# The gated rows of a state-space scan: both tiles interleaved in a job of one step per chunk, with a scratch row for each tile

## What is computed

```python
y = y + d_skip[:, None] * xs
y = y.reshape(B, S, SSD_WIDTH) * silu(sz)                  # the gate
y_ssd = rms_norm(y.reshape(B, S, SSD_GROUPS, gsz), ssd_norm.reshape(SSD_GROUPS, gsz))
```

## Time and profile before

| | us |
|---|---|
| median of 3 runs (lowest to highest) | 3448.64 (3448.18 to 3449.01) |
| the profiled execution, device time | 3450.18 |
| its span in the trace | 3448.4 |
| PE busy / DVE busy / ACT busy | 3332.8 / 2236.4 / 1704.1 |
| mean granted PE clock | 0.984 |
| DMA moved, mean rate | 719.32 MB, 209 GB/s |

### The profile page before, as it was taken

One profiled execution on the slowest core, in us unless ns is written; L12 is line 12 of the kernel. 1 busy time (PEld: TensorE's weight loads), 2 busy tenths in 40 slices (PEclk: granted clock), 3 DMA queues, 4 the chain that ended last, 5 costly groups with the idle time before them and its releaser, 6 DMA issues.

```text
span 3448.4 us, 43913 instructions
## 1 busy us (share of the span) xinstructions
PE 3332.8 (97%) x18250; PEld 2894.4 (84%) x18250; DVE 2236.4 (65%) x2687; ACT 1704.1 (49%) x2098; POOL 46.8 (1%) x90
## 2 busy tenths in 40 slices
PE   5899999999999999999999999999999999999998
PEld 5779978888888887899788878888898899988887
DVE  5788777866667556776666576655567776544444
ACT  3355565554434344656646544344447775434343
POOL 0000000000000000000000000000000000000000
PEclk8799999999999999999999999999999999999999
DMA  9764456567777555444444467765555443455553
GB/s 367 274 228 170 167 226 245 218 228 259 263 277 295 208 183 183 175 168 160 172 182 159 176 239 270 265 250 192 189 184 191 182 165 135 166 216 194 194 187 142
DMA packets 102918, 719.32 MB, mean 209 GB/s; under 512 B 12176, under 2 KB 12256, under 8 KB 18752
## 3 DMA queue, kind: packets, MB, share of 16 engines
q1 hardware_dynamic: 93888, 675.38, 53.6%
q0 software_dynamic: 8256, 37.64, 3.1%
q10 hardware_dynamic: 576, 3.50, 0.3%
HBM read 710.08 MB, written 6.40 MB: 208 GB/s over the span
## 4 chain that ended last, share of the span: by engine, by line
PE 87%; DVE 7%; ACT 3%; issue 1%; DMA 1%; SPq 0%; DVEq 0%; ACTq 0%
PE G L1214 80%; DVE LL L1812 3%; DMA RAW<-w_ada_turned_packed_dram 1%; PE BD L1335 1%; PE BA L1362 1%; DVE S L2019 1%; PE BD L1397 1%; DVE RAW L1823 1%; ACT HH L1455 1%; PE BC L1348 1%; PE BE L1280 0%; PE BA L1416 0%; PE BC L1416 0%; PE BC L1380 0%; ACT WW L1734 0%
## 5 line engine op out<-in xcount | busy, mean ns | idle before, releaser
L1455 ACT ACTIVATE HH<-RAW 128x2048 fp32r<-128x2048 f32 x546 | 1044.8, 1914 | 1071.4 <-PE G L1214 1017.1
L1812 DVE TENSOR_TENSOR LL<-RAW,HH 128x2048 fp32r<-128x2048 f32 x546 | 1248.1, 2287 | 362.3 <-ACT HH L1455 361.9
L1214 PE MATMUL G<-HH,UH 128*128 128x512 f32 x2560 | 1021.1, 399 | 51.0 <-DVE LL L1812 46.7
L1214 PE MATMUL G<-HH,UL 128*128 128x512 f32 x2560 | 1003.2, 392 | 0.0
L1214 PE MATMUL G<-LL,UH 128*128 128x512 f32 x2560 | 1003.0, 392 | 0.0
L1214 PEld LDWEIGHTS G<-HH,UH 128*128 128x128 f32 x2560 | 484.7, 189 | 159.6 <-DVE LL L1812 56.2
L1214 PE MATMUL G<-UH,HH 128*128 128x256 f32 x2080 | 603.0, 290 | 10.2 <-DVE XS L2055 7.7
L1214 PE MATMUL G<-UH,LL 128*128 128x256 f32 x2080 | 589.3, 283 | 0.0
L1214 PE MATMUL G<-UL,HH 128*128 128x256 f32 x2080 | 589.1, 283 | 0.0
L1214 PEld LDWEIGHTS G<-LL,UH 128*128 128x128 f32 x2560 | 484.4, 189 | 103.3
L1214 PEld LDWEIGHTS G<-HH,UL 128*128 128x128 f32 x2560 | 485.2, 190 | 100.5 <-issue 2.9
(11 more groups left out here) (336 smaller groups left out, 2304.7 us busy)
## 6 DMA issues: line engine op xcount, KB each, us to landing
RAW<-in_w_in_packed_dram SPq DMA_DIRECT2D x402, 1024.0 KB, 4.8
RAW<-w_ada_turned_packed_dram SPq DMA_DIRECT2D x88, 1024.0 KB, 5.0
RAW<-in_w_out_packed_dram SPq DMA_DIRECT2D x48, 1024.0 KB, 4.8
RAW<-in_w_o_ssd_packed_dram SPq DMA_DIRECT2D x32, 1024.0 KB, 4.8
RAW<-in_w_o_fox_packed_dram SPq DMA_DIRECT2D x16, 1024.0 KB, 4.8
RAW<-in_w_o_dsa_packed_dram SPq DMA_DIRECT2D x16, 1024.0 KB, 5.7
RAW<-in_w_proj_a_packed_dram SPq DMA_DIRECT2D x16, 1024.0 KB, 4.8
RAW<-in_w_proj_b_packed_dram SPq DMA_DIRECT2D x16, 1024.0 KB, 4.7
```

The lines of the kernel that those rows point to most:

```text
L1214: mm = pe.matmul(to, lt, rh, start=first, stop=end, skip_group_check=True)
L1455: a.activation(HH[g % NH][:, :n], RAW[buf(ch["f"])][:, :n], ACT.Copy).then_inc(*hi_done.up(g))
L1812: v.tensor_tensor(LL[buf(f)][:, :n], RAW[buf(f)][:, :n], HH[g % NH][:, :n].bitcast(F32), ALU.subtract).then_inc(*lo_done.up(g))
```

## The change

The job `sz` still has five steps, none of them with MID. The two tiles go one behind the other: gate 0; gate 1 and norm 0; norm 1 and the transposes of 0; store 0 and the transposes of 1; store 1. After gate 1 the block's banks are declared free with sz_y of tile 1. Tile 1 gets its own scratch row XD in place of S1 and its own two columns of SM2, so that its gate waits for no event of the lane; its transposes wait until tile 0 has been stored, since both go through BE.

```diff
--- before.py
+++ after.py
@@ -407,15 +407,20 @@
     def sz(l, g):
         def steps(b):
             o.tok_block["sz", l, g] = b
-            for t in range(2):
-                put("sz_gate", l, g, t)
-                yield
-                put("sz_norm", l, g, t)
-                yield MID
-                put("sz_turn", l, g, t)
-                yield
-                put("sz_put", l, g, t)
-                ended("sz_done", l, g, t)
+            put("sz_gate", l, g, 0)
+            yield
+            put("sz_gate", l, g, 1)
+            o.blocks[b]["free_by"] = ("sz_y", l, g, 1)
+            put("sz_norm", l, g, 0)
+            yield
+            put("sz_norm", l, g, 1)
+            put("sz_turn", l, g, 0)
+            yield
+            put("sz_put", l, g, 0)
+            put("sz_turn", l, g, 1)
+            yield
+            put("sz_put", l, g, 1)
+            ended("sz_done", l, g, 1)
         return steps
 
     def gate(key):
@@ -874,6 +879,7 @@
     TURN = [(BA, BC), (BD, BE)]
     MT = [(BA, BC), (BD, BE), (BA, BC), (BD, BE)]
     SS = [S1, S2]
+    ZZ = [S1, XD]
     CV = [S1, S2]
     ROT = {"rot": (0, 16), "idx": (32, 8)}
     LW = [XD[:, :], XDD[:, :]]
@@ -1313,6 +1319,8 @@
 
         def sz_turn(l, g, t):
             pe.wait_ge(*sz_normed.at(l, g, t))
+            if t:
+                pe.wait_ge(*sz_done.at(l, g, 0))
             y = xsK[:, g, t, :]
             for j in range(4):
                 mm = pe.transpose(BE[:, j * P:(j + 1) * P], y[:, j * P:(j + 1) * P], ident)
@@ -1590,14 +1598,15 @@
         def sz_gate(l, g, t):
             b = o.tok_block["sz", l, g]
             a.wait_ge(*multiplied(b))
-            a.wait_ge(*evac_before("sz_gate", l, g, t))
-            a.activation(S1[:, :], GB[o.blocks[b]["set"]][t][:, :], ACT.Tanh, scale=0.5).then_inc(*sz_tanh.up(l, g, t))
+            if t == 0:
+                a.wait_ge(*evac_before("sz_gate", l, g, t))
+            a.activation(ZZ[t][:, :], GB[o.blocks[b]["set"]][t][:, :], ACT.Tanh, scale=0.5).then_inc(*sz_tanh.up(l, g, t))
 
         def sz_norm(l, g, t):
             a.wait_ge(*sz_y.at(l, g, t))
-            a.activation(S1[:, :], xsK[:, g, t, :], ACT.Square, accum_out=SM2[:, 0:1]).then_inc(*sz_sum.up(l, g, t))
+            a.activation(ZZ[t][:, :], xsK[:, g, t, :], ACT.Square, accum_out=SM2[:, 2 * t:2 * t + 1]).then_inc(*sz_sum.up(l, g, t))
             a.wait_ge(*sz_sum.at(l, g, t))
-            a.activation(SM2[:, 1:2], SM2[:, 0:1], ACT.Sqrt, bias=EPT[:, 0:1],
+            a.activation(SM2[:, 2 * t + 1:2 * t + 2], SM2[:, 2 * t:2 * t + 1], ACT.Sqrt, bias=EPT[:, 0:1],
                          scale=1.0 / 512).then_inc(*sz_root.up(l, g, t))
 
         def gate(key, t):
@@ -2037,17 +2046,18 @@
             bk = GB[o.blocks[o.tok_block["sz", l, g]]["set"]][t]
             y = xsK[:, g, t, :]
             v.wait_ge(*sz_tanh.at(l, g, t))
-            v.scalar_tensor_tensor(S1[:, :], S1[:, :], 1.0, bk[:, :], ALU.add, ALU.mult).then_inc(*own.up())
+            v.scalar_tensor_tensor(ZZ[t][:, :], ZZ[t][:, :], 1.0, bk[:, :], ALU.add, ALU.mult).then_inc(*own.up())
             v.wait_ge(*own.last())
             v.wait_ge(*ssd_yd.at(l, g, 1))
-            v.scalar_tensor_tensor(y, S1[:, :], 0.5, y, ALU.mult, ALU.mult).then_inc(*sz_y.up(l, g, t))
+            v.scalar_tensor_tensor(y, ZZ[t][:, :], 0.5, y, ALU.mult, ALU.mult).then_inc(*sz_y.up(l, g, t))
 
         def sz_norm(l, g, t):
             y = xsK[:, g, t, :]
             v.wait_ge(*sz_root.at(l, g, t))
-            v.reciprocal(SM2[:, 1:2], SM2[:, 1:2]).then_inc(*own.up())
+            r = SM2[:, 2 * t + 1:2 * t + 2]
+            v.reciprocal(r, r).then_inc(*own.up())
             v.wait_ge(*own.last())
-            v.tensor_scalar(y, y, SM2[:, 1:2], None, ALU.mult).then_inc(*sz_normed.up(l, g, t))
+            v.tensor_scalar(y, y, r, None, ALU.mult).then_inc(*sz_normed.up(l, g, t))
 
         def sz_put(l, g, t):
             y = xsK[:, g, t, :]
```

## The result

The changed kernel takes 3442.89 us (median of 19 runs, 3441.05 to 3444.63); the kernel before, run beside it on the same chip, 3449.01 (19 runs, 3447.26 to 3452.74). The ratio is 0.9983, 95% interval 0.9976 to 0.9989: faster by 0.17%, 6.1 us. The interval leaves out 1, so the gain is clear of the spread of the runs, and it lies inside the 0.2% that the prediction called no difference, close to its edge. The forecast was 3442.4. The profiled execution has a span of 3441.1 us (before 3448.4) and a mean granted clock of 0.984 (before the same).

A forecast was written before the change was run, and what follows sets the result against it. PE, busy 97% of the span, was taken as the bound. From 3450.18 us profiled, -16.5 (old stalls) + 5.95 (layer 0) + 4.4 (layer 1) = -6.2, and -1.54 to the median, gave 3442.4 us; own range 3439 to 3446, wider range 3431 to 3451.

The forecast's parts named there:

- no difference: Whole kernel: times between 3441.7 and 3455.5 us, within 0.2% (6.9 us), count as the same; chance 0.50.
- The old stalls: PE's six waits on the second tile's store go: 10.0 us in layer 0, 6.5 in layer 1, together 16.5.
- Chunk 97 without slack: Chunks 97 and 294: gate's multiplies ready 4.1 us into a chunk of 5.5; cost 0, bound 2.2 us.
- rival D: Second step, six groups: packed work makes subtractions late, 2.2 us each plus lower clock, 3459.0 us; chance 0.16.
- 0, at most 0.3: Tile 1's transposes, moved to a chunk's end, wait for tile 0's store: no cost, at most 0.3 us in group 0.
- The new stall at chunk 101 and 298: PE waits for silu's second half: 4.25 us plus 1.7 of lower clock, 5.95 in layer 0.
- granted clock near 0.5: Sign of being right: clock near 0.5 behind the idle of about 4.2 us ahead of chunks 101 and 298.
- The second stall of layer 1: Ahead of chunk 300, through rope and table loads: PE waits 3.8 us more; layer 1 pays 4.4 us in all.
- The table load: Loads in layer 1: 1.28 us without drain; with the page's 1380 ns drain, 2.8 us longer, about 3445.2.
- The sum: Whole kernel: -16.5 + 5.95 + 4.4 = -6.2 us, giving 3442.4 us.
- rival C: Silu stalls come but the clock holds: -8.5 us, 3440.1 us; chance 0.14.
- the 0.57 ahead of chunk 93: Layer 0's middle old stall: two idles close together, clock 0.57 over 4 us behind them, 1.7 us lost.

The follow-up runs named there:

- e2: The changed kernel with one yield less, so that the job has four steps for four chunks; 3434.49 us, ratio 0.9959.
- e10c: e7 with one scratch row for both tiles instead of two; 3430.38 us, ratio 0.9946.
- e6: The changed kernel with one scratch row for both tiles instead of two; 3447.32 us, ratio 0.9993.
- e8: The changed kernel with sixteen empty side steps instead of two ahead of rope in layer 1, five-step job kept; 3438.93 us, ratio 0.9968.
- e7: e2 with sixteen empty side steps instead of two ahead of the rope and parameter steps in layer 1; 3425.68 us, ratio 0.9931.
- e1: The changed kernel without the line that sets free_by, the early release of the banks; 3441.39 us, ratio 0.9978.
- e3: The changed kernel with both silu halves of the fg blocks in one step, five-step job kept; 3438.07 us, ratio 0.9970.
- e5: The kernel before, old tile order kept, with only the early release (free_by = sz_y of tile 1) added; 3453.44 us, ratio 1.0011.
- e4: The changed kernel with two more empty side steps ahead of rope in layer 1; 3442.23 us, ratio 0.9982.

## Why the prediction came out right, step by step

**The old stalls.** Predicted 10.0 us in layer 0 and 6.5 in layer 1. Chunk 80 to chunk 100 gives 9.8 us, chunk 270 to chunk 297 gives 6.4; e2 gives 9.7 and 6.2. The waits are gone, as said.

**Chunk 97 without slack.** Predicted: the pair of multiplies is ready 4.1 us into chunk 96, no stall. Chunk 96 starts at 743.24; DVE's second multiply of tile 1 ends 4.10 us later, and chunk 97 starts at 749.00 without an idle:

```profile
746.65 0.69 DVE L2052 SCALAR_TENSOR_TENSOR XS<-XD,XS 128x512 f32<-128x512 f32 x1
...
748.75 2.29 DVE L1821 TENSOR_TENSOR LL<-RAW,HH 128x2048 fp32r<-128x2048 f32 x1
```

**The packed second step (rival D).** The subtraction behind that step was put at some 5 us into the chunk, with 3 to 4 us of slack. Ahead of chunk 97 it begins at 748.75, 5.5 us in, is over at 751.04, and chunk 98, for which it is, starts at 755.11: 4.1 us. D's mechanism did not occur in the changed kernel. It was not far away: 1.33 us more in that step, in the four-step kernel, brought it about once (e10c, chunk 87). And e6 and e10c show how near another place was that I had costed at "0, at most 0.3": tile 1's transposes in group 0. By themselves they cost little. Chunks 84 and 281 start 0.44 and 0.45 us later against the kernel before, but 0.3 of it is back one chunk on, since a set of transposes has only changed its place, and PE shows no idle there. With one scratch row the delay ahead of them is paid in full.

**The new stall at chunk 101 and 298.** Predicted an idle that makes 4.25 us, and 1.7 of lower clock, 5.95. Measured idle 4.08 us, the clock 0.68 and 0.66 for 5 us (1.6 and 1.7 us), and 5.75 and 5.94 us between the two chunks on either side. The order of events is the one forecast: the last matmul of chunk 100 starts at 772.78, then ACT copies for chunk 103 and only then comes the tanh of silu's second half, and DVE's second multiply releases PE at 777.14.

```profile
773.15 1.91 ACT L1463 ACTIVATE HH<-RAW 128x2048 fp32r<-128x2048 f32 x1 [1.93 <-PE G L1220]
774.97 0.58 ACT L1565 ACTIVATE S<-G 128x512 f32<-128x512 f32 x1
```

```profile
776.31 0.69 DVE L2018 SCALAR_TENSOR_TENSOR QQ<-S,QQ 128x512 f32<-128x512 f32 x1
```

The sign "granted clock near 0.5" was half right: the lower level held for about two thirds of the 5 us.

**The second stall of layer 1.** The chain through rope and the tables was worked out step by step from E, the end of chunk 297 (here 1961.34, its start, plus the 5.76 that it takes, 1967.1). DVE and ACT in order of time:

```profile
1973.47 0.21 DVE L1885 TENSOR_SCALAR WW<-WW 128x96 f32<-128x96 f32 x1
...
1985.22 2.28 DVE L1821 TENSOR_TENSOR LL<-RAW,HH 128x2048 fp32r<-128x2048 f32 x1
```

```profile
1973.71 0.28 ACT L1501 ACTIVATE RT<-WW 128x96 f32<-128x96 f32 x1 [2.66 <-DVE WW L1885]
1974.01 1.28 ACT L1565 ACT_TABLE_LOAD   x1
1975.31 0.60 ACT L1565 ACTIVATE S<-G 128x512 f32<-128x512 f32 x1
```

First rope part done at 6.6 (predicted 6.7), tanh begins at 8.2 (8.3, over by 8.9), the subtraction for chunk 300 is over at 20.4 (20.6), PE starts at 20.5 (20.7); idle 3.46 (3.8). The lower clock comes a second time behind it, 0.66 for 5 us, 1.7 us, as counted, and from chunk 301 on PE goes at 5.44 us a chunk without an idle: DVE hides (its subtraction for chunk 304 is over 1.3 us before the chunk starts; the forecast had 1.7). Chunk 304 is reached at 44.0 (predicted 44.3), and layer 1 pays 4.0 us from chunk 297 to 304 (predicted 4.4).

**The table load.** The rows show again a load of 1.28 us with tanh right behind it, and the load itself 0.02 us behind the end of Sin. The Trainium skill, "ScalarE: Activation LUTs", section "What ACT_TABLE_LOAD costs", has about 1380 ns of drain beside 1283 ns of load; the load agrees, and of the drain nothing is to be seen here. The median lies at 3442.9 and not at the 3445.2 that I had worked out from that page. The load of Sin, in turn, started before its operand was there (at 1969.77, the Sin itself waited until 1973.71), so only the way back to tanh was on the path.

**The sum.** By rows of the table the change is worth -4.0 in layer 0 (chunk 80 to 102) and -2.5 in layer 1 (chunk 270 to 306), -6.5 together; predicted -6.2. The medians differ by 6.1. In the sum itself no term was off by more than half a microsecond, and these partly cancel. One figure beside it was wrong: without the lower clock layer 1 would pay 20.7 + 21.9 - 39.9 = 2.7 us by the prediction's own steps, not the 3.7 given there, so rival C should have stood at 3439.1 and not at 3440.1; the forecast does not use it. What was right beyond luck is the mechanism: e2 takes both new stalls away, e8 the second alone, e7 what e2 leaves, and each comes within 2 us of its forecast. That the time was met to half a microsecond is in part luck. The forecast counts 1.7 us of lower clock behind each new idle, and the same 4.08 us cost 1.5 and 1.7 us of clock here and 2.4 and 2.8 in e6. The expectations of e1, e3, e5 and e6 missed by 2 to 5.4 us, all with too low a time. What the traces don't settle is the rest between spans and medians: against the kernel before, the profiled runs of e1, e3, e5 and e8 differ from the medians by 1.4 to 3.1 us, of which about 1 us is that the profiled run of the kernel before lies above its median.

## What to carry to other kernels

Count the slots of a job against the chunks that it has. A job of five steps for blocks of four chunks was kept in time by the very waits that the change removed; an early release without a step fewer only passes the debt on to the next job that has none (here silu, worth 8.4 us), and with a step fewer the release was worth nothing. And look at what else uses the lane at the place to which the debt moves: two rope parts and a table load between two tanh made the second stall of the changed kernel, and in the four-step kernel the same side steps, moved by eleven chunks, gave another 8.8 us, more than the change itself. The four steps have a price too: between chunks 83 and 98 several subtractions are over only 1.0 to 1.3 us before they are needed (chunks 87, 90, 94), where the changed kernel has 1.9 us or more at every chunk, so less can still be put into them.

## What the runs showed of the hardware

The lower clock behind an idle of PE is not decided by the idle's length alone. In the stretches of the change it stayed at 1.00 behind 1.90 us twice (e3), and behind 3.46 us and more it fell each time (0.50 to 0.71 over 5 us). In between it went both ways at the same place: ahead of chunk 304 the kernel before idles 2.15 us and e2 2.13 us, after the same instructions.

Stretches of the kernel before and of e2 behind this idle:

```profile
2018.00:2023.00 5.00, 5.00 (x22) 4.11 (x23) 5.00 (x7) 1.95 (x2) 0.00 (x0) 1.00 0.50 210
```

```profile
2001.40:2006.40 5.00, 4.98 (x15) 3.96 (x16) 5.00 (x7) 2.03 (x2) 0.00 (x0) 0.66 0.55 231
```

e1 and e4 fell there as well (0.66, 0.67). It is worth 1.5 to 1.6 us each time, and it explains half of the 3 us by which e1 fell short and nearly all of e2's 1.7 (3434.5 for 3432.8).

Nor is 1.90 us a length below which the clock is safe. Outside the change, ahead of chunk 260, all twelve traces have the same idle of 1.54 us after the same instructions; behind it the clock is 0.66 over 5 us in four of them (the changed kernel, e3, e4, e6) and 1.00 in the other eight. The changed kernel and e2:

```profile
1724.95 0.50 PE L1220 MATMUL G<-HH,UH 128*128 128x512 f32 x1 [1.54 <-DVE LL L1821]
```

```profile
1725.00:1730.00 5.00, 5.00 (x18) 4.04 (x19) 3.59 (x4) 1.52 (x1) 0.00 (x0) 0.66 0.32 134
```

```profile
1720.79 0.50 PE L1219 MATMUL G<-HH,UH 128*128 128x512 f32 x1 [1.54 <-DVE LL L1820]
```

```profile
1720.80:1725.80 5.00, 5.00 (x29) 4.32 (x30) 3.63 (x4) 1.55 (x1) 0.00 (x0) 1.00 0.35 147
```

That is where a column of the table moves by 1.6 us between chunks 102 and 270 without the change having a part in it. Nor does it take two idles close together, as the prediction read the 0.57 ahead of chunk 93: in e5 that chunk has a single idle of 2.24 us and the clock is 0.66, while the kernel before has 2.24 us ahead of chunk 89 and stays at 1.00. What decides it stays open.

The two idles of 4.08 us show the same spread: 0.68 and 0.66 in the changed kernel, 0.50 in e6 at both, where 2.4 and 2.8 us were lost instead of 1.5 and 1.7.
